# Four pieces of a decoder layer's instruction order: probabilities, transposes, value sets and key decay moved

## The reference, cut to what matters

```python
z = einsum(rmsnorm(x, norm_g), w_in)             # 3584 columns: rq rk rv rg | mq mk mv
# A: retention, 4 heads of 128, chunks of 128
scores = einsum(qc, kc) * decay_in
inner, cross = scores @ vc, (qc * q_dec) @ s
s_new = chunk_dec * s + (kc * k_dec).T @ vc
# B: block-sparse attention, 8 heads of 64; decode tokens see 2048 cached keys in 8 blocks of 256
gate = einsum('qhd,hnd->qhn', q, k_mean)         # top 3 past blocks + own block
p = softmax(scores of the chosen blocks);  out = p @ v
hres = x + concat(norm(ret) * silu(rg), out) @ w_out
# C: 32 experts, top 4 per token, SwiGLU
acc += g * (swiglu(tok @ w_gate_up + b) @ w_down + b_down)      # for each expert
y = rmsnorm(hres + acc, final_norm_g)
```

## Time and profile before

| | |
|---|---|
| time, median of 3 runs | 1240.31 us (1240.19 to 1242.56) |
| profiled execution: own time / span | 1238.33 us / 1236.5 us |
| mean granted TensorE clock | 0.994 of full |
| PE busy | 1195.6 us (97%) |
| DVE / ACT / POOL busy | 389.5 / 234.0 / 68.0 us |
| DMA | 500.64 MB, mean 405 GB/s |

### The profile page before, as it was taken

The page is one execution under the profiler, slowest core; times in us unless marked ns, Lnnn a source line. Parts: engine busy times, 40 slices in busy tenths (PEclk is TensorE's granted clock), DMA queues, the critical chain, the costliest instruction groups (busy, mean ns, idle before and its releaser), DMA issues.

```text
span 1236.5 us, 17233 instructions
## 1 busy us (share of the span) xinstructions
PE 1195.6 (97%) x7264; PEld 507.2 (41%) x7264; DVE 389.5 (32%) x554; ACT 234.0 (19%) x521; POOL 68.0 (6%) x70
## 2 busy tenths in 40 slices
PE   7999999999999999999999999999999999999996
PEld 3555544535443434344343434343343434343432
DVE  4999956464311111222111111112111111111113
ACT  4021145304111101021211101021202111111103
POOL 2222202230000000000000000000000000000000
PEclk9999999999999999999999999999999999999999
DMA  8999889999999999999999999999999999999995
GB/s 333 369 363 361 332 326 389 382 363 385 381 414 427 428 428 428 429 428 428 430 427 430 427 429 428 428 429 428 429 428 429 429 428 430 428 428 430 426 430 233
DMA packets 49978, 500.64 MB, mean 405 GB/s; under 512 B 5656, under 2 KB 6320, under 8 KB 19088
## 3 DMA queue, kind: packets, MB, share of 16 engines
q1 hardware_dynamic: 42416, 430.56, 83.3%
q0 software_dynamic: 7520, 69.47, 14.2%
HBM read 495.29 MB, written 4.72 MB: 404 GB/s over the span
## 4 chain that ended last, share of the span: by engine, by line
PE 66%; DMA 21%; DVE 8%; issue 4%; ACT 1%; SPq 0%; DVEq 0%; ACTq 0%
PE psum L1027 24%; DMA arena<-w_gate_up 18%; PE psum L1058 14%; PE psum L935 6%; DVE arena L1556 5%; DMA arena<-w_down 3%; PE psum L533 3%; PE psum L955 3%; PE psum L941 2%; PE psum L967 2%; PE psum L624 2%; PE psum L753 2%; PE psum L453 2%; PE psum L974 1%; PE psum L1094 1%
## 5 line engine op out<-in xcount | busy, mean ns | idle before, releaser
L1027 PE MATMUL psum<-arena 128*64 128x512 f32 x1920 | 421.7, 594 | 11.8 <-DMA arena<-w_gate_up 11.8
L1027 PEld LDWEIGHTS psum<-arena 128*64 128x64 f32 x1920 | 135.0, 137 | 294.9 <-issue 267.5
L1899 DVE TENSOR_SCALAR arena<-psum 128x512 f32<-128x512 f32 x32 | 22.2, 692 | 675.2 <-PE psum L1027 635.9
L1058 PE MATMUL psum<-arena 128*64 128x512 f32 x960 | 212.6, 595 | 0.0
L1184 ACT ACTIVATE arena<-psum 128x512 f32<-128x512 f32 (+4 forms) x192 | 97.6, 511 | 350.4 <-PE psum L1058 170.6
L1556 DVE STREAM_TRANSPOSE arena<-arena 128x2048 f32<-128x2048 f32 x32 | 121.4, 3926 | 2.1 <-PE psum L518 1.9
L1058 PEld LDWEIGHTS psum<-arena 128*64 128x64 f32 x960 | 66.2, 136 | 124.3 <-issue 122.5
L533 PE MATMUL psum<-arena 128*128 128x512 f32 x224 | 107.7, 618 | 0.4 <-ACT arena L1184 0.4
L1429 ACT ACTIVATE arena<-arena 128x512 f32<-128x512 f32 x30 | 18.9, 631 | 412.5 <-DVE arena L1899 412.5
L1184 ACT ACTIVATE arena<-psum,arena 128x128 f32<-128x128 f32 (+2 forms) x162 | 49.3, 404 | 174.1 <-PE psum L533 113.7
L935 PE MATMUL psum<-arena 128*128 128x128 f32 x512 | 76.8, 293 | 0.2 <-DVE arena L1811 0.2
(11 more groups left out here) (261 smaller groups left out, 705.0 us busy)
## 6 DMA issues: line engine op xcount, KB each, us to landing
arena<-w_gate_up SPq DMA_DIRECT2D x128, 2048.0 KB, 31.1
arena<-w_down SPq DMA_DIRECT2D x63, 2048.0 KB, 33.0
arena<-w_in SPq DMA_DIRECT2D x7, 2048.0 KB, 25.1
arena<-w_out SPq DMA_DIRECT2D x2, 2048.0 KB, 12.8
out<-arena POOLq DMA_DIRECT2D x1, 2048.0 KB, 19.5
arena<-w_down SPq DMA_DIRECT2D x2, 1024.0 KB, 38.8
out<-arena SPq DMA_DIRECT2D x3, 512.0 KB, 4.6
arena<-x_prompt SPq DMA_DIRECT2D x2, 512.0 KB, 5.5
```

Source lines behind the costliest of these rows:

```text
L1027: last = mm(psum[64 * g:64 * (g + 1), b, :], xt[:, 2 * kk + m, lhs], gate_slot[slot][:, m, c:c + 512], start=False, stop=kk == 3 and m == ...
L1058: last = mm(psum[64 * g:64 * (g + 1), 2, :], at_sb[:, m, SLOTS * q:SLOTS * (q + 1)], down_slot[slot][:, m, 512 * g:512 * (g + 1)], start=q ...
```

## The change

Only the order of instructions changes; none is added or taken away, and the work is the same.

```diff
--- before.py
+++ after.py
@@ -648,12 +648,14 @@
                 mark[f"o_t{g}"] = (d_full, n)
 
             prompt_part(5, 0)
-            prompt_part(5, 1)
+            p_transposes(0, 0)
+            p_transposes(0, 1)
+            prompt_part(5, 1, 0)
             n_rv = sample_part(5)
             mark["block5"] = (a_full, A.n)
             mark["z5"] = [(a_empty, n_rv)]
-            p_transposes(0, 0)
-            p_transposes(0, 1)
+            p_transposes(0, 2)
+            p_transposes(0, 3)
             own_transposes(0)
             for u in range(6):
                 V.wait_empty(pe)
@@ -665,14 +667,9 @@
                               mq_t[r:r + 64, h // 2, tile * P:(tile + 1) * P],
                               mk_t[r:r + 64, h // 2, 0:w], start=True, stop=True)
                 V.filled(last)
-                if u == 1:
-                    p_transposes(0, 2)
-                    p_transposes(0, 3)
-                elif u == 3:
-                    value_set(0)
-            value_set(1)
-            prompt_part(6, 0, 2)
-            value_set(3)
+                if u % 2:
+                    value_set((u + 1) // 2)
+            prompt_part(6, 0)
             prompt_part(6, 1, 4)
             n_rg = sample_part(6)
             mark["block6"] = (a_full, A.n)
@@ -1316,12 +1313,15 @@
             evacuate_block(z[:, 1], 1)
             evacuate_scores(7)
             evacuate_sample(z[0:NS, 1, 2, :])
+            probabilities(0)
             evacuate_block(z_rv)
-            probabilities(0)
+            evacuate_pt(0, 0)
+            evacuate_pt(0, 1)
             evacuate_block(z_rv, 1)
             evacuate_sample(z_rv[0:NS, 2, :])
-            for part in range(4):
-                evacuate_pt(0, part)
+            evacuate_pt(0, 2)
+            evacuate_pt(0, 3)
+            evacuate_sequence(0)
             act.wait_ge(p_bias, 1)
             for b in range(MH):
                 ins = nc.scalar.activation(s_prompt[:, b, :], s_prompt[:, b, :], ACT.Exp,
@@ -1332,16 +1332,15 @@
                 ins = nc.scalar.activation(s, s, ACT.Exp, bias=pm[:, 24 + h:25 + h], scale=SCALE,
                                            accum_out=pm[:, 40 + h:41 + h])
             ins.then_inc(p_exp, 1)
-            evacuate_sequence(0)
             evacuate_block(z_rg)
             evacuate_block(z_rg, 1)
             evacuate_sample(z_rg[0:NS, 2, :])
             evacuate_sequence(2)
             for u in range(0, 6, 2):
                 evacuate(pt_prompt[:, 4 * u:4 * u + 4, :].rearrange("p b t -> p (b t)"))
+            probabilities(1)
             A.wait_full(act)
             A.emptied(copy(mix_t[:, 4:6, 0:LP], psum[:, A.bank(), :].rearrange("p (c w) -> p c w", c=2)))
-            probabilities(1)
             evacuate_pt(1, 0)
             evacuate_pt(1, 1)
             evacuate_t(rq_t, 0)
@@ -1692,8 +1691,8 @@
             s1 = s_prompt[:, 8:24, :].rearrange("p (h b) t -> p h (b t)", h=8)
             v.tensor_tensor(s1, s1, pm[:, 56:64].unsqueeze(2).broadcast_to([P, 8, LP]), ALU.mult)\
                 .then_inc(p_probs, 1)
+            evacuate_sequence(1)
             choose(1)
-            evacuate_sequence(1)
             for u in range(1, 6, 2):
                 evacuate(pt_prompt[:, 4 * u:4 * u + 4, :].rearrange("p b t -> p (b t)"))
             V.wait_full(dve)
@@ -1703,15 +1702,15 @@
             own_reciprocal(1)
             evacuate_own(1)
             normalise(0)
+            evacuate_t(rq_t, 1)
+            evacuate_t(rk_t, 1)
+            evacuate_t(rk_t, 2)
             for semaphore, value in mark["prompt_o"]:
                 dve.wait_ge(semaphore, value)
             dve.wait_ge(mv_stored, 32)
             dve.wait_ge(mvs_ready, 1)
             v.tensor_tensor(k_dec, rot_k, kd.unsqueeze(3).broadcast_to([P, TILES, RH, P]),
                             ALU.mult).then_inc(kdec_ready, 1)
-            evacuate_t(rq_t, 1)
-            evacuate_t(rk_t, 1)
-            evacuate_t(rk_t, 2)
             heads_to_mix(0)
             dve.wait_ge(qdm_zero, 1)
             V.wait_full(dve)
```

## The result

| | before | changed |
|---|---|---|
| time, median | 1240.47 us (20 runs, 1238.12 to 1245.82) | 1245.08 us (20 runs, 1240.02 to 1368.03) |
| ratio, 95% interval | | 1.0027 [1.0015, 1.0039] |
| profiled execution: time / span | 1238.33 / 1236.5 us | 1243.81 / 1242.0 us |
| mean granted clock | 0.994 | 0.991 |

The one run of 1368.03 us had a granted clock of 0.85 and is not in the ratio. By the ratio the change costs 3.3 us (1.9 to 4.8); the medians differ by 4.6. I had predicted 1239.0, a gain of 1.3 us, and a range of 1236.9 to 1242.9: it is slower instead, and outside the range. Of the other 19 runs six took 1240.0 to 1241.4 us and thirteen 1243.8 to 1249.1.

What follows compares the result with a forecast made beforehand. The expert stage's weight stream over full DMA engines sets the end, its start set by the first stage's PE, ACT, DVE chain. Reordering +0.4 us and clock -1.7 total -1.3: 1239.0 us from 1240.3, range 1236.9 to 1242.9.

Steps and rivals of the forecast that it cites:

- The end follows the start of pair 0 one for one: Expert stage: a later start of the first expert pair delays the end equally; an earlier one gains up to 2.4 us.
- Edit 1: Block 5: probabilities(0) ahead of the block copies, two transpose groups between tiles; net +1.7 us, bounds 0.3 to 3.0.
- Edit 2: Score units: value sets placed amid them; DVE's delay mostly hidden before the transposes; +0.1 us, bounds 0 to 0.8.
- Edit 3: Near 213 us: probabilities(1) ahead of the mix copy, so PE's 1.42 us wait for exponentials goes; -1.4 us.
- Edit 4: Key decay (`k_dec`) behind the turned copies: taken as 0; the old order would cost up to 0.7 us at full clock.
- The clock: PE's half-speed stretch from 217.1 to 220.4 us should go with the 1.42 us idle time before it: -1.7 us.
- The rule of the Trainium skill: Transposes don't count as busy like matmuls, so the fall at 217.1 us stays: +0.4 us, 1240.7 us; chance 22%.
- The state: Rival: PE waits for the retention state, landing about 233.7 us; gives back at most 1 us, 1240.0 us; chance 6%.

Runs made afterwards that it cites:

- run 36: Not a run number: the words are "in this run" and "36 transposes"; the run is the changed kernel's profiled execution, all four reorderings against the kernel before, 1243.81 us.
- the kernel with edits 1 and 2: Kernel before with only the first group's probabilities and transposes inside block 5 and value sets amid the score units: 1242.57 us, ratio 1.0014.
- run 7: Changed kernel with four further 128x512 matmuls, result unused, where PE goes on to wait for the retention state: 1244.99 us, ratio 1.0054.

## Why the prediction was wrong, step by step

- **The end follows the start of pair 0 one for one: right.** Span less start of pair 0 (by the chain) is 921.0 us before and 922.8 changed (the fall in the tail is the 1.7 between them), 920.4 to 922.9 in the runs above, for starts from 312 to 330.
- **Edit 1, +1.7: right.** Idle 0.96 and 0.30 us (1.0 and 0.3), the table load at 153.5, tile 1 9.66 us behind the start of the block (9.8 in the forecast, 7.0 before): +2.66 - 1.16 = +1.5.
- **Edit 2, +0.1: too small, within its bounds.** PE waits 0.68 us for DVE's first copies, which stand behind `choose(1)`. I had both engines at the bank within 0.2 us of each other and took the kinder side. PE is done with value set 7 at 214.66, 62.4 us after block 5, before at 213.05, 60.2: +2.3 for edits 1 and 2, against +1.8.
- **Edit 3, -1.4: right.** No idle time ahead of the transposes at 214.66.
- **Edit 4, 0: right for its own wait**, with its 0.7 us if the order had stayed. That the same 0.7 us also brings set 11 nearer to the state had no term.
- **The clock: half right.** The fall at 217 went, and with it the 1.7 us. The rule of the Trainium skill that I weighed ("TensorE: Matmul & The Clock Gate", Part 4) would have let it stay; in this run 36 transposes in a row went at a granted clock of 1.00 (window 218.10 to 222.40). But my reason, the idle time of 1.42 us, is not shown: the kernel with edits 1 and 2 had the same idle time and no fall, so that this fall went may be luck. I had no term for falls elsewhere, and there were three.
- **The state: the step that failed.** I held it for 6% and "at most 1 us of the 1.3". The sum was made as "It lands 20.6 us after its issue": a landing read from one row and moved along with its issue, to 233.7, and set against the 235.13 of the first product that reads the state, while the wait stands 0.35 us ahead of it, at the products that begin at 234.78. It took 22.5 us and came at 235.5, where PE stood from 233.43 on. The kernel with the later issue showed that the landing does not follow the issue, and the one with the held gather that the packets of set 11 are what delays it. Edit 3 and the clock, my two gains, bring the request for set 11 nearer by 3.1 us. The wait was 2.2 us and the fall right behind it 1.7: 3.9 where I had at most 1. Without it, in the kernel with half of the state, pair 0 stood where before had it within 0.5 us and the time was 1.5 us under before. Up to the wait the sum of the terms came out: forecast -1.3, measured -0.7, and the 0.5 between them are those of edits 1 and 2 (2.3 against 1.8). The falls at 264 and in the tail have counterparts in kernels without the wait; that they fell into the profiled execution of the changed kernel and not of the one before is chance as far as the traces tell.

That the thirteen slower runs of the changed kernel are those in which the state came late, and the six faster ones those in which it was in time, fits with the profiled run of 1243.81 us and the scatter in run 7, but each kernel has one trace: argued, not shown. Nor is it shown why the last packets are left on one engine.

## What to carry to other kernels

A transfer's time to landing is no property of the transfer: where the DMA engines are full, work out what runs beside it, and above all in which gap its small packets get through, before you move anything that sets the gap. A gain on the engine that asks for the next large load is also an earlier competitor for every small load in flight. A spare time of 3 us ahead of a reader, on a queue that shares full engines, is worth a rival of its own: here the wait came to 2.2, 5.3 and 13.9 us where I had allowed for one.

## What the runs showed of the hardware

- Packets of 2 KB and of 16 KB on two queues pass one for one (90 and 91 in 4 us), though they cost 0.11 and 0.63 us. 2 MB in small packets took 12.9 to 34.3 us to land.
- The last of such a load can hang on one engine: with 15 of 16 counts in at 232.6 and 237.6 us the last came at 235.5 and 244.9, its packets 0.73 us apart.
- Issued by POOL, whole, the same load landed after 13.2 to 18.4 us, in packets of 4 KB, behind or ahead of a gather in the same queue.
- Whole falls of the clock make up much of the scatter of single runs. Of 29 runs of the kernel before in one comparison, the 13 with a mean granted clock of 0.994 took 1239.2 us in the mean, the 6 with 0.990 1242.5: 3.3 us, about what two falls cost.
- A fall does not follow from the length of one idle time: 1.42 us had one behind it in the kernel before and in the one with the later state, none in the one with edits 1 and 2; 2.20 us had one, 1.0 and 1.6 us none.
- A fall in the tail, 3.4 us at half speed, stood in 14 of the 17 traces, whatever the first stage did.
